# Step 1's first tile: ranking in four rounds of two heads, gathers waiting round by round

## The reference, cut to what matters

```python
def block(xb):                                   # 128 tokens
    q = (xb @ w_q).reshape(T, H, 2, PEER_QDIM // 2)          # H = 8
    s = jnp.einsum('thpc,pnc->thpn', q, sub_keys)            # 128 keys in each of 2 halves
    top_s, top_i = lax.top_k(s, K)                           # K = 16
    cand_s = top_s[:, :, 0, :, None] + top_s[:, :, 1, None, :]
    cand_i = top_i[:, :, 0, :, None] * PEER_N_KEYS + top_i[:, :, 1, None, :]
    best_s, best_j = lax.top_k(cand_s.reshape(T, H, K * K), K)
    idx = jnp.take_along_axis(cand_i.reshape(T, H, K * K), best_j, axis=-1)
    g = jax.nn.softmax(best_s, axis=-1)
    u, v = expert_u[idx], expert_v[idx]                      # gathered rows of 1024
    act = jax.nn.gelu(jnp.einsum('thkd,td->thk', u, xb), approximate=False)
    return jnp.einsum('thk,thkd->td', g * act, v)
```

## Time and profile before

| | |
|---|---|
| median of 3 runs | 3788.93 us (3781.67 to 3794.72) |
| profiled execution, its own time | 3789.43 us |
| its span | 3787.6 us |
| mean granted clock of TensorE | 0.862 |
| busy: TensorE, VectorE, GpSimd, ScalarE | 77%, 60%, 30%, 18% |
| DMA over the span | 345 GB/s mean, 1308.57 MB |

### The profile page before, as it was taken

How to read it: one execution, slowest core, us unless ns; L and a number is a source line. 1 busy time by engine, 2 the same in 40 slices (tenths; PEclk the granted TensorE clock), 3 DMA queues, 4 the chain that set the end, 5 groups by cost and what they waited for, 6 DMA issues and landing times. The chain is left out here.

```text
span 3787.6 us, 31946 instructions
## 1 busy us (share of the span) xinstructions
PE 2901.6 (77%) x11208; PEld 1477.7 (39%) x11208; DVE 2273.8 (60%) x5605; ACT 682.6 (18%) x1250; POOL 1153.4 (30%) x1044
## 2 busy tenths in 40 slices
PE   6689894689988876789988876788998845555555
PEld 3358661345644422345644422344563511111111
DVE  1230168776454888775454887776455688665665
ACT  1220011541111112531111112441111000000000
POOL 0000003443332333333333233332332325443442
PEclk9779996899998988899998977898998966777777
DMA  4125548899999999899999999889999969999998
GB/s 156 54 61 160 174 151 351 352 416 396 397 418 401 390 361 397 342 372 385 398 418 390 382 376 375 352 351 362 401 418 400 397 234 395 421 421 386 420 421 367
DMA packets 213745, 1308.57 MB, mean 345 GB/s; under 512 B 25537, under 2 KB 26321, under 8 KB 82001
## 3 DMA queue, kind: packets, MB, share of 16 engines
q0 software_dynamic: 149760, 1082.20, 70.5%
q1 hardware_dynamic: 63824, 224.33, 16.3%
HBM read 1292.80 MB, written 13.63 MB: 345 GB/s over the span
## 5 line engine op out<-in xcount | busy, mean ns | idle before, releaser
L608 POOL DMA_INDIRECT rowbuf<-in_peer_uv,idx x875 | 977.9, 1118 | 2214.3 <-PE acc L874 1475.2
L874 PE MATMUL acc<-rowbuf,diag 128*64 128x512 f32 x3500 | 1051.3, 714 | 443.4 <-DVE diag L1505 437.7
L1495 DVE CUSTOM_DVE_ANT_0 rowbuf<-rowbuf,xr 128x1024 f32<-128x1024 f32 x875 | 1049.9, 1222 | 402.3 <-DMA rowbuf<-in_peer_uv,idx 400.1
L874 PEld LDWEIGHTS acc<-rowbuf,diag 128*64 128x64 f32 x3500 | 254.9, 155 | 1051.3 <-DVE diag L1505 578.2
L1113 ACT ACTIVATE acts<-dots 128x2 f32<-128x2 f32 x512 | 104.0, 203 | 2337.3 <-DVE dots L1495 2245.0
L1505 DVE TENSOR_SCALAR diag<-consts,acts,gw 128x64 f32<-128x64 f32 x1024 | 285.3, 350 | 225.4 <-ACT acts L1113 101.0
L667 PE MATMUL bank<-xnT,W 128*128 128x256 f32 x1792 | 410.2, 385 | 0.0
L653 PE MATMUL bank<-W,xnT 128*128 128x512 f32 x832 | 377.9, 605 | 3.1 <-DVE xnT L1201 2.6
L667 PEld LDWEIGHTS bank<-xnT,W 128*128 128x128 f32 x1792 | 338.3, 192 | 91.9 <-issue 47.9
L667 PE MATMUL bank<-arena,W 128*128 128x256 f32 x1024 | 248.5, 402 | 38.3 <-DMA W<-in_w_blocks 35.9
L874 PE MATMUL acc<-kv,diag 128*64 128x512 f32 x468 | 176.0, 771 | 108.5 <-DVE diag L1505 98.4
(11 more groups left out here) (168 smaller groups left out, 2295.3 us busy)
## 6 DMA issues: line engine op xcount, KB each, us to landing
W<-in_w_blocks SPq DMA_DIRECT2D x360, 512.0 KB
rowbuf<-in_peer_uv,idx POOLq DMA_INDIRECT x875
xs<-in_x SPq DMA_DIRECT2D x16, 512.0 KB
xr<-x SPq DMA_DIRECT2D x32, 256.0 KB
out_y<-xs SPq DMA_DIRECT2D x8, 512.0 KB, 8.2
x<-arena SPq DMA_DIRECT2D x8, 512.0 KB
fin<-out_y POOLq DMA_DIRECT2D x8, 512.0 KB
out_y<-fin POOLq DMA_DIRECT2D x8, 512.0 KB, 16.6
```

Source lines behind the costliest of these rows:

```text
L608: pool.indirect_dma_start(rows[SLOT[g]], None, a["peer_uv"], bass.IndirectOffsetOnAxis(ap=idx[:, at // NB, at % NB:at % NB + 1], axis=0)). ...
L874: mm = pe.matmul(acc[HP * j:HP * (j + 1), h * HALF:(h + 1) * HALF], diag[:, c % DIAGS, j, :], v[:, D + h * HALF:D + (h + 1) * HALF], start ...
L1495: dve.tensor_tensor_reduce(out=u, in0=u, in1=xr[:, t, j, :], scale=1.0, scalar=0.0, op0=ALU.mult, op1=ALU.add, accum_out=dots[:, c % QS, j ...
```

## The change

`places_of(1)` interleaves the score blocks with ranking rounds for tile 0: WQ0, SC0, round 0, WQ1, SC1, round 1, WQ2, both XT, SC2, round 2, WQ3, SC3, round 3, then K, V, both KT and Q of step 2, the ranking of tile 1 with QT in it. Each round has two places, R(1,0,2j) and R(1,0,2j+1). Round j ranks heads 2j and 2j+1 of tile 0. Picks become due from R(1,0,4), the third round, on. The total number due by R(2,1,0) is as before. `routed` gives the new counts of `route_done`, which runs to 4 for tile 0. Steps 2 to 4 keep their order.

```diff
+ROUNDS = HEADS // 2
+FIRST_PICK = ("R", 1, 0, 2 * 2)
+def routed(n, t, j=ROUNDS - 1):
+    if n == 1:
+        return ROUNDS + 1 if t else j + 1
+    return ROUNDS + 1 + NT * (n - 2) + t + 1
...
+    if n == 1:
+        ranks = [[("R", n, 0, 2 * j), ("R", n, 0, 2 * j + 1)] for j in range(ROUNDS)]
+        last = [("R", n, 1, i) for i in range(RANKS)]
+        out += [("WQ", n, 0), ("SC", n, 0)] + ranks[0] + [("WQ", n, 1), ("SC", n, 1)] + ranks[1]
+        out += [("WQ", n, 2), ("XT", n + 1, 0), ("XT", n + 1, 1), ("SC", n, 2)] + ranks[2] + [("WQ", n, 3), ("SC", n, 3)] + ranks[3]
+        f = front(n + 1)
+        return out + f[:5] + last[:2] + f[5:] + last[2:]
...
-    starts = [places.index(("R", m, 1, 0)) for m in range(1, STEPS + 1)]
+    starts = [places.index(FIRST_PICK if m == 1 else ("R", m, 1, 0)) for m in range(1, STEPS + 1)]
...
+        first = oT_xa.rearrange("p a b -> p (a b)")
+        hot_1 = parts(first[:, 0:512], 2, TOPK, TOPK)
...
-                sp.wait_ge(route_done, NT * n)
+                sp.wait_ge(route_done, routed(n, 1))
...
-                    pool.wait_ge(route_done, NT * (n - 1) + t + 1)
+                    if n + t > 1:
+                        pool.wait_ge(route_done, routed(n, t))
                     first = NT * NB * (n - 1) + NB * t
                     for k in range(NB):
+                        if n + t == 1 and k % (NB // ROUNDS) == 0:
+                            pool.wait_ge(route_done, routed(n, t, k * ROUNDS // NB))
```

On TensorE each score block follows its own WQ block in step 1, where it followed the next one. On ScalarE each round's exponentials come before the copy of the next WQ block, and the gelu of pick 0 moves to round 2:

```diff
+                if n == 1:
+                    for j in range(4):
+                        if j < 2:
+                            act.wait_ge(x2_out[j], 16 * n)
+                        copy(("WQ", n, j), qp[:, j % 2, :], 1024)
+                        if j == 1:
+                            square_x(n + 1)
+                        scores(j)
+                        if j == 1:
+                            scale_x(n + 1)
+                        if j == 2:
+                            gelu(0)
+                        ranked_round(j)
+                    return
```

On VectorE `begin` of step 1 moves behind the third top-16 and each round behind its own; `rank` takes the round as j, its arrays and slices narrowed to two heads, the one-hot lookup done once for two heads in place of twice for four:

```diff
-                          [(order[j], 0.4), (order[j], 0.8)] if j < 2 else [])
+                          [(order[j], 0.4), (order[j], 0.8)] if j < 2 and n > 1 else [])
                     dve.memset(st2[:, 7:8], 0.0).then_inc(top_done, 1)
+                    if n == 1:
+                        if j == 2:
+                            begin(n)
+                        rank(n, 0, j)
...
-                rank(n, 0)
+                if n > 1:
+                    rank(n, 0)
...
+            def rank(n, t, j=None):
                 def part(i):
-                    picks.upto(("R", n, t, i))
+                    picks.upto(("R", n, t, i if j is None else 2 * j + i // 3))
+                heads = slice(0, HEADS) if j is None else slice(2 * j, 2 * j + 2)
+                nh = heads.stop - heads.start
+                hot, cand, bv, bj, tif = tables if j is None else tables_1
...
+                halves = 2 if j is None else 1
                 for s in range(2):
-                    for half in range(2):
+                    for half in range(halves):
                         if s or half:
                             part(1 + 2 * s + half)
```

More of the change, by code:

```diff
@@ L859, in route @@
                     channel_major(("WQ", n, j), xn2T)
+                    if n == 1:
+                        if j == 2:
+                            turn_x(n + 1)
+                        score(j)
+                        continue
                     if j:
@@ L863, in route @@
                         turn_x(n + 1)
-                score(3)
+                if n > 1:
+                    score(3)
             def add(c):
@@ L1422, in route @@
                     finish(n - 1, 1)
-                begin(n)
+                if n > 1:
+                    begin(n)
                 rank(n, 1)
-            def rank(n, t):
+            tables, tables_1 = (hot, cand, bv, bj, tif), (hot_1, cand_1, bv_1, bj_1, tif_1)
+            def rank(n, t, j=None):
                 def part(i):
-                    picks.upto(("R", n, t, i))
+                    picks.upto(("R", n, t, i if j is None else 2 * j + i // 3))
+                heads = slice(0, HEADS) if j is None else slice(2 * j, 2 * j + 2)
+                nh = heads.stop - heads.start
+                groups = slice(2 * heads.start, 2 * heads.stop)
+                hot, cand, bv, bj, tif = tables if j is None else tables_1
+                b = bf[:, :, heads, :]
@@ L1459, in rank @@
+                after(dve.tensor_tensor(flat(b[:, 1, :, :]), flat(b[:, 1, :, :]), flat(b[:, 2, :, :]), ALU.add))
+                halves = 2 if j is None else 1
                 key = tif.rearrange("p (h two) k -> p h two k", two=2)
                 for s in range(2):
-                    for half in range(2):
+                    for half in range(halves):
                         if s or half:
                             part(1 + 2 * s + half)
[L1464 to L1468, removed]
+                        hh = slice(half * nh // halves, (half + 1) * nh // halves)
+                        after(dve.tensor_tensor(hot, wide(b[:, s, hh, :].unsqueeze(3), nh // halves, TOPK, TOPK),
+                                                wide(iota.unsqueeze(1).unsqueeze(1), nh // halves, TOPK, TOPK), ALU.is_equal))
+                        after(dve.tensor_tensor(hot, hot, wide(key[:, hh, s, :].unsqueeze(2), nh // halves, TOPK, TOPK), ALU.mult))
+                        ins = dve.tensor_reduce(flat(b[:, 2 + s, hh, :]), hot.rearrange("p h a b -> p (h a) b"), AX, ALU.add)
@@ L1469, in rank @@
                         after(ins)
                 part(5)
-                for j in range(2):
+                here = slice(TOPK * heads.start, TOPK * heads.stop)
+                for half in range(2):
                     for h in range(2):
-                        i1, i2 = (flat(bf[HP * j:HP * (j + 1), w, :, :]).rearrange("p (i a) -> p a i", a=2)[:, h, :] for w in (2, 3))
-                        dve.scalar_tensor_tensor(idx[HP * h:HP * (h + 1), t, :].rearrange("p (i j) -> p j i", j=2)[:, j, :], i1, float(NKEY), i2,
+                        i1, i2 = (flat(b[HP * half:HP * (half + 1), w, :, :]).rearrange("p (i a) -> p a i", a=2)[:, h, :] for w in (2, 3))
+                        dve.scalar_tensor_tensor(idx[HP * h:HP * (h + 1), t, here].rearrange("p (i j) -> p j i", j=2)[:, half, :], i1, float(NKEY), i2,
@@ L1475, in rank @@
                                                  ALU.mult, ALU.add)
[L1476 to L1479, removed]
+                dve.wait_ge(sm_exp, routed(n, t, ROUNDS - 1 if j is None else j))
+                after(dve.tensor_reduce(b[:, 6, :, 0], b[:, 4, :, :], AX, ALU.add))
+                after(dve.reciprocal(b[:, 6, :, 1], b[:, 6, :, 0]))
@@ L1480, in rank @@
+                for half in range(2):
                     for h in range(2):
[L1481 to L1484, removed]
+                        tok = slice(HP * half, HP * (half + 1))
+                        ins = dve.tensor_tensor(gw[HP * h:HP * (h + 1), t, here].rearrange("p (e i j) -> p j e i", j=2, i=TOPK // 2)[:, half, :, :],
+                                                b[tok, 4, :, :].rearrange("p e (i a) -> p a e i", a=2)[:, h, :, :],
+                                                wide(b[tok, 6, :, 1].unsqueeze(2), nh, TOPK // 2), ALU.mult)
```

50 lines of the change are left out of this document (31 added, 19 removed).

## The result

The changed kernel took 3797.99 us in the median of 20 runs (3786.61 to 3804.77), the kernel before 3786.22 us in 20 (3777.52 to 3800.4). The ratio is 1.0028, 95% interval 1.0018 to 1.0038: 10.6 us slower, 7 to 14. The forecast was 4 us faster. The time lies inside the range, but the sign is wrong, and the loss is clear of noise though it is about the 11 us that I had set as the edge of "the same".

The account below looks back on a forecast made before the run. The prediction took transport of gathered rows by DMA to bound nearly all the time after a late start, though not alone. A return of 58 us against a lag of 54 gave -4 us on 3789.43: 3785 us, range 3757 to 3814.

Parts of the forecast that it names:

- The shift at R(2,1,0): Steps 2 to 4 keep their code, so the shift at about 1422 us goes to the end undiminished.
- Section 3: Step 1 to step 2's first scores: dense work lags 48 us, 54 with the clock, bounds 40 to 75.
- the walk: Event-by-event timetable of VectorE and TensorE in step 1: `queries` possible at 642.8 us, second ranking with eight picks at 701.
- The last leg: From step 1's second ranking to step 2's first scores: same chain, one pick lighter (-3 us), ending at 756 us.
- the clock's 6: TensorE at half clock after stops in WQ3 and K adds 6 us to the lag, from nothing to 20.
- the upper bound of 20 us: Clock loss if half of WQ3, K, V and Q runs at 1.2 GHz and nothing hides it.
- Section 4: From step 2's first scores to R(2,1,0): 14.7 fewer picks give back 58 us, summed by stretch.
- My two bounds: Return of 14.7 fewer picks: 73 us if DMA sets all of it, 28 us if TensorE does.
- Section 2: In step 1 twelve gathers run ahead into free row buffers; the first pick moves from about 591.6 us to the third round.
- a check from the other side: At 756 us, 32 picks done instead of 27: 25 us of DMA in front; other limits 15 and clock 6 leave 4.
- (a): Rival: DMA sets the pace all through, 73 us come back, lag near 48: -25 us, 3764; chance 0.32.
- (b): Rival: TensorE and VectorE stop each other from WQ3 to Q(2), lag 70 to 80: +12 to +28 us, middle 3808; chance 0.28.

Follow-up runs that it names:

- e4: Changed kernel with its first gathers held until the second round is done, picks as in the changed kernel: +9.5 us against the kernel before.
- e1: Changed kernel with picks due from R(1,1,0), as before the change; rounds, score order and early gathers stay: +6.1 us against the kernel before.
- e2: Changed kernel with picks due from K(2), behind all four rounds: +2.6 us against the kernel before (-3 to +9).
- e11: Changed kernel with picks due from K(2) and gathers held until the second round is done: +3.8 us against the kernel before (-1 to +9).
- e7: e1 with gathers held until all four rounds are done and the first two dots behind `queries`: 0 us against the kernel before (-4 to +4).
- e9: e5 with gathers held until tile 0 is ranked and first two dots behind `queries`: 3772.76 us against 3781.58 for the kernel before, ratio 0.9974.
- e10: Kernel before with score blocks behind their WQ blocks, four rounds in one piece after top-16s and `keys`, gathers waiting round by round: +4.5 us against before.
- e5: e1 with WQ copies ahead of the exponentials, next x before the second round, K normalized before the fourth: -3.8 us against the kernel before.
- e6: e5 with picks due from K(2): +15 us against the kernel before (+10 to +20).

## Why the prediction was wrong

**Right.** First gather at 497.5 us (502.63 less the 5.2 of the opening), 83 us earlier. A round is 11.6 us (490.11 to 501.74). The fixed cost per instruction of the earlier trace rows carries to 128x32 and 128x512 (0.19 and 0.69 us), as the Trainium skill's measured term has it (VectorE: DVE Perf Modes, section on the TRN2 errata). TensorE stops inside WQ3 and in K, and VectorE idles before `queries`, at the forecast places, if not for as long: 8.5 us after WQ3's first quarter where I had some 20, 14.8 before `queries` where I had 20. The shift at R(2,1,0) passes to the end undiminished: 9.1 and 9.2 us. Lag and return nearly cancel; the sum just has the other sign.

**Section 3, the lag: 54 forecast, 63.1 measured.** This is the step that failed most, in two terms. (1) A stand of VectorE of 5.9 us in the second round, which the walk did not have. At the ranking of tile 1 the walk gives 210.5 after the norm (`queries` at 642.8 and 10 us more make 204.5, and the clock's 6), measured 213.9, and 210.2 with the stand away (e4). That e4 meets the walk is partly luck, since the two idle times were shorter than forecast. (2) The last leg, from there to the first scores of step 2, was to take 103 us and took 109.6. It is the larger term: in e4, without the stand, the first scores came only 1.4 us sooner. I had made it 3 us shorter for one pick less and taken 55 us for its second part; measured from the last write of `gw` plus its pick it was 60, in the kernel before 59. In that leg VectorE waits in turn for ScalarE and TensorE (4.93, 6.30, 5.08 and 4.00 us, and 4.44 at its end) while DMA is not full (share 0.71 from 750 to 800 us); that one pick more or less in it changes nothing fits, but no run tried it.

The clock's share was there. The first quarter of WQ3 took 5.99 us for 16 instructions (its last quarter, behind dense work, 3.72), and pick matmuls after the stops 3.68 or 3.21:

```profile
530.47 5.99 PE L693 MATMUL bank<-arena,W 128*128 128x256 f32 x16 [4.31 <-DVE xnT L1254]
544.93 3.68 PE L906 MATMUL acc<-rowbuf,diag 128*64 128x512 f32 x8 [8.47 <-DVE diag L1574]
555.27 3.68 PE L906 MATMUL acc<-rowbuf,diag 128*64 128x512 f32 x8 [6.66 <-DVE diag L1574]
558.88 7.21 PE L693 MATMUL bank<-arena,W 128*128 128x256 f32 x32
...
567.89 3.72 PE L693 MATMUL bank<-arena,W 128*128 128x256 f32 x16
...
588.97 3.68 PE L906 MATMUL acc<-rowbuf,diag 128*64 128x512 f32 x8 [8.20 <-DVE diag L1574]
592.58 2.24 PE L679 MATMUL bank<-W,xnT 128*128 128x512 f32 x4
599.43 3.21 PE L906 MATMUL acc<-rowbuf,diag 128*64 128x512 f32 x8 [4.61 <-DVE diag L1574]
```

`queries` began 203.7 us after the norm, 9.4 later than the walk without the clock; less the stand that is 3.6, and in e4, which has no stand there, it is 5.8. I had put 6. The Trainium skill's rule (TensorE: Matmul & The Clock Gate, Part 1: half clock is the default and activity releases it) agrees with these rows, but not my reading of it that the upper bound of 20 us was the nearer: the picks that refill TensorE release it again.

**Section 4, the return: 58 forecast, 54.0 measured.** By stretch: 9.6 (9 forecast), 8.6 (12), 18.0 (12), 11.3 (19), 6.5 (6). The merge gave more than I took, all that DMA's price allows (16) and more, though TensorE was full. The stretch from 800 to 941 us gave 3 less and the one behind the merge 8 less; in both DMA's share had fallen (0.93 and 0.96) and TensorE had time left. I priced picks with one mean of 3.9 us; in this order the first lot gave 4.8 and the second 2.1 (e1, e2, changed; 2.8 between e11 and e4), while the lag cost 3.4 to 4.2 at every pick. That is why a balance of means came out near zero for a set of picks whose second half loses. My two bounds, DMA or TensorE sets the pace, missed that a stretch can be held with neither full; by what is not shown.

**Section 2** gave the early gathers no cost and "a check from the other side" took five picks as 25 us in front. The first is refuted: e7 and e9 show that they cost 6 us where picks stay (with the dots set early), and e4 that 22 us of them are worth nothing that can be measured. Twelve buffers are all that an early gather can fill. The second left out that it takes DMA being full all the way to turn picks in front into time.

**Rivals.** (a), DMA sets the pace, is out: 73 us were to come back. (b) named the right place, but its lag of 69 was not reached; it was right in sign and gave half in size. R(2,1,0) came at 1430.9 us by the clock of the kernel before, between the forecast's 1425 and the 1436 of (b). Of my own theory after the result (picks ahead of dense work are the whole loss) e1 took a part away: without them there are still 6 us.

**Open.** What VectorE stands for. I had called it a fetch of instructions. The queues by window show instruction packets between 495 and 503 us and none from 503 to 530 in the changed kernel, so no row shows such a fetch at the stand. The Trainium skill (Runtime: NRT & Kernel Launch, section on instruction fetch mechanics) has engines fetch their program in blocks of 16 KB through DMA, mostly hidden; that would fit that e4 and e10 have early gathers and no stand, but it is only argued. Why the early gathers cost 6 us at the end in e1 and e5, where the stand is 5.8 and 7.9 us, while e4 won only 1 to 3 us by its absence, also stays open, and so does what lengthened the second stretch.

## What to carry to other kernels

An earlier start of the stream that bounds a kernel is worth what its buffers let it do: price the consumer that frees them, not the first transfer. Where work is spread over a fixed order, price the next unit of shift and not the mean, and look stretch by stretch at what comes back: here most of the shortfall lay where neither DMA nor TensorE was full. And when parts of a ranking are pulled into an earlier stage, look at each in-order engine for what they were put in front of: three changes of order were worth 10 us here (e1 to e5, e7 to e9), as much as the whole change lost.

## What the runs showed of the hardware

VectorE stood up to 2.5 us at a time, 4.6 to 7.9 us in all, for no data and no semaphore that the trace shows, from 9 to some 17 us after the first of a burst of indirect transfers, in six kernels (changed twice, e1, e2, e5, e6, e11). The instructions at which it stands differ by kernel; the first of them was the same in the two traces of the changed kernel. In e5 and e6 one such gap was 6.99 and 6.27 us, and in e5 ScalarE's copy of WQ2 began 2.7 us after TensorE had filled it, against 0.2 in e9. In the kernels whose burst came later (e4, e7, e9, e10) there was none above 0.7 us.

The unchanged code up to the norm differed by up to 6.7 us between the fourteen traces, 6.4 of it within the first 110 us, as much as many of the effects looked for here; only places counted from a common instruction, or many runs, tell them apart.
